# Modulation blocks loaded from GpSimd's queue, a second buffer in the third mixer's stage, and their sums spread anew over VectorE's program

## The chip, the core and the metric

The program runs on one core of a Trainium2 chip. The metric is the device time of one execution in microseconds; before the change it was 1848.09 us, the median of three runs (1843.42, 1848.1 and 1848.09).

## The reference

A sequence of 256 latent tokens (width 1024) goes through two blocks of two layers each. Only layer code of the first block matters here. 256 context tokens go with it in its first layer; the second layer drops their output.

```python
mod = c_silu @ ada_w + ada_b                     # one row for the latents
mod_c = cctx_silu @ ada_w + ada_b                # one row for the context
shift, scale, gate = jnp.split(mod, 3, axis=-1)
hx = rmsnorm(x, norm_w) * (1 + scale) + shift
px = split_cols(hx @ w_in)
ya = global_gqa(...)          # mixer A
yb = neighbourhood_attn(...)  # mixer B
yc_ = window_gqa(...)         # mixer C
ux = concatenate([ya, yb, yc_]) * silu(px[9])
x = x + gate * (ux @ w_out)
```

Everything is float32. The second block (a SwiGLU, two sparse attentions, a merge, a SwiGLU, twice) isn't touched.

## The kernel before

TensorE multiplies float32 operands as two halves: ScalarE rounds a weight panel to a high part (`round_half`, L1019), VectorE subtracts it for the low part (`split_half`, L1581), and three products give the result. A panel is 128x2048 floats (1 MB); raw, high and low panels have two buffers each. SyncE's queue loads the raw panels in order; each load waits until the low part of the panel two before it has been made. The order of the work on each engine is written out by hand, and semaphores tie the engines together.

A layer of the first block runs mixer A, B, C. Each has projections (`qkv`), the output product of the mixer before it (`wout`), a gate (`gate`), turns of queries and keys by transposes, and attention.

A modulation tile is 128 of the 3072 columns of `mod`. TensorE makes the 16 tiles of the first layer's shift and scale at the start; the other 32 of both layers (`MOD_TILES`) are made on VectorE. The weights of one tile are a block `modw[i]` of 128x1024 floats (512 KB). A tile takes two sums, one with the latents' row and one with the context's: a multiplication with a running sum over 1024 columns (`mod_sums`, L1743), whose products go to PSUM banks 4 to 7. The rows (`c_rows`, 128x2048) are loaded first and passed through silu by ScalarE (L1212). There are three phases (`MOD_PHASES`): B0 in mixer B of the first layer (tiles 0 to 15), C0 in mixer C of the first layer (16 to 23) and B1 in mixer B of the second layer (24 to 31). `MOD_AT` says how many sums stand at which place of VectorE's program: after the split of a projection panel (`panel1`), between copies of queries and keys (`near0`, `near2`), after a turn by the position tables (`turned1`), after a residual step of `wout` (`out0` to `out3`), in the gate (`gate0`).

Three readers wait for sums. TensorE waits before the turns of C0 (L2877) until all sums of C0 are there, and in attention B (L2683) until those of B are, since both want banks 4 to 7. The residual of mixer A's output product (`wout`, L2163) waits for gates of its layer. TensorE takes a pair of banks again (`take`, L2445) only when the residual of the step two before it has read them. So a residual that is late on VectorE holds TensorE.

The blocks are loaded by SyncE's queue among the panels (`mod_load`, L866): in B0 and B1 in turn into two halves of `token_major`, in C0 into one buffer in `near_bias`, with a wait until the sums of the block that lies there are made. GpSimd's own queue loads the near mixer's bias tables (`near_bias`, L944).

Of the kernel before, what the change touches and what calls it, by code (L numbers as in the profile page):

```python
# [29 lines left out]
ALU = mybir.AluOpType  # L30
# [3 lines left out]
P = 128  # L34
D = 1024
KT = D // P
T = 256
# [28 lines left out]


MOD_AT = {("B", 0): {"near0": (0, 3), "panel1": (3, 6), "panel2": (6, 8), "near2": (8, 11), "panel3": (11, 14), "panel4": (14, 17),
                     "panel5": (17, 20), "out0": (20, 22), "out1": (22, 24), "out2": (24, 26), "out3": (26, 28),
                     "gate0": (28, 30), "gate1": (30, 32)},  # L70
          ("C", 0): {"panel1": (0, 2), "turned1": (2, 4), "panel2": (4, 6), "turned2": (6, 8), "out0": (8, 10), "out1": (10, 12),
                     "out2": (12, 14), "out3": (14, 16)},
          ("B", 1): {"near0": (0, 1), "panel1": (1, 3), "panel2": (3, 5), "near2": (5, 8), "panel3": (8, 10), "panel4": (10, 13),
                     "panel5": (13, 16)}}
# [242 lines left out]
def program(nc, ctx, xin, smallg, small1, small2, consts, rpb, crows, modw, weights, out):  # L317
# [3 lines left out]
    def sem(name):  # L321
        return ctx.enter_context(nc.semaphore(name))
# [69 lines left out]
    mod_in, mod_sum = [sem(f"modulation_weights_in{i}") for i in range(3)], sem("modulation_sums_done")  # L392
# [168 lines left out]
    def c_rows(m):  # L561

        return tok[:, K1:K1 + 2 * D] if m == "B" else gates[:, :]

    def mod_weights(m, i):

        return tok[:, i % 2 * D:(i % 2 + 1) * D] if m == "B" else bias[:, 0:D]

    def mod_landed(m, i):

        if m == "C":
            return mod_in[2], 16 * (i - MOD_PHASES["C", 0][0] + 1)
# [271 lines left out]
    def _(sp):  # L844
# [22 lines left out]
        def mod_load(m, i):  # L867

            first = MOD_PHASES[m, 0][0] if i < 24 else 24
            held = 2 if m == "B" else 1  # L870
            if i - first >= held:
                sp.wait_ge(mod_sum, 2 * (i - held + 1))
            sp.dma_start(mod_weights(m, i), modw[i]).then_inc(mod_landed(m, i)[0], 16)

        def c_rows_load(m, l):

            if m == "B":
                before = ONE["attnA", l]
                sp.wait_ge(pv, before.at["groups"] + before.groups)
            else:  # L880
                before = ONE["attnB", l]
                sp.wait_ge(omul, before.at["pairs"] + before.pairs)
            row = bass.AP(crows.tensor, crows.offset, [[0, P], [1, 2 * D]])
            sp.dma_start(c_rows(m), row).then_inc(c_rows_in, 16)
            for i in range(2 if m == "B" else 1):
                mod_load(m, MOD_PHASES[m, l][0] + i)

        mod_loads = {}
        for (m, l), counts in (("B", 0), (1, 2, 2, 2, 1, 3, 2, 1)), (("B", 1), (0, 1, 3, 1, 1)), (("C", 0), (0, 2, 3, 2)):
            n, i = ONE["qkv" + m, l].at["panels"] + 2, MOD_PHASES[m, l][0] + (2 if m == "B" else 1)  # L890
            for k, count in enumerate(counts):
                mod_loads[n + k] = [(m, i + j) for j in range(count)]
                i += count
            assert i == MOD_PHASES[m, l][1], (m, l, i)

        for n in range(ADA_FIRST + 1, START2["panels"] + 2):
            before = 4 if n == ADA_FIRST + 1 else n - 2
            for m, l in MOD_PHASES:
                if before == ONE["qkv" + m, l].at["panels"] + 2:
                    c_rows_load(m, l)  # L900
            freed_panel(before)
            sp.dma_start(raw_of(n, 0, PAN), weights[n]).then_inc(loaded[n % 2], 16)
            for m, i in mod_loads.get(before, ()):
                mod_load(m, i)
# [28 lines left out]
    def _(pool):  # L933
# [10 lines left out]
        def near_bias(l, i):  # L944
# [7 lines left out]
                pool.wait_ge(mod_sum, 2 * MOD_PHASES["C", 0][1])  # L952
            pool.dma_start(near_buffer(i % 3), rpb[l * NPAIR * TT + i]).then_inc(bias_in[i % 3], 16)

        def add_a(k, j):

            pool.wait_ge(sqa_ready, now(sqa_ready, 4 * (k - 1) + j + 1))
            pool.tensor_tensor(squares_a(0), squares_a(0), squares_a(j), ALU.add).then_inc(pool_chain, 1)
            pool.wait_ge(pool_chain, chain.next())
# [6 lines left out]
            pool.tensor_tensor(squares_b(0), squares_b(0), squares_b(j), ALU.add).then_inc(pool_chain, 1)  # L966
            pool.wait_ge(pool_chain, chain.next())

        for i in range(NPAIR * TT):
            near_bias(0, i)  # L970
        near_bias(1, 0)
        near_bias(1, 1)
        add_a(1, 1)
# [12 lines left out]
        for kt in range(KT):  # L986
            half = x_normed(kt)[:, T:2 * T]
            pool.tensor_tensor(half, half, invb, ALU.mult).then_inc(ctx_ready, 1)
        for i in range(2, NPAIR * TT):
            near_bias(1, i)  # L990
        assert chain.n == POOL_ENTRY, chain.n
# [579 lines left out]
    def _(dve):  # L1571
# [12 lines left out]
        def split_panel(n):  # L1584
            split_half(n, 0)
            split_half(n, 1)
# [143 lines left out]
        def mod_sums(m, l, a, b):  # L1730


            for x in range(a, b):
                i, v = MOD_PHASES[m, l][0] + x // 2, x % 2
                layer, tile = MOD_TILES[i]
                if x == 0:
                    dve.wait_ge(c_rows_silu, 2 * (list(MOD_PHASES).index((m, l)) + 1))
                dve.wait_ge(*mod_landed(m, i))
                add = sm1[:, layer * NSMALL1 + SMALL1["ada_b"][0] + tile:layer * NSMALL1 + SMALL1["ada_b"][0] + tile + 1]
                to = mod[:, layer * 48 + 2 * tile + v:layer * 48 + 2 * tile + v + 1]  # L1740
                if x >= 2:
                    dve.wait_ge(mod_sum, 2 * MOD_PHASES[m, l][0] + x - 1)
                dve.tensor_tensor_reduce(mod_products(x), mod_weights(m, i), c_rows(m)[:, v * D:(v + 1) * D], 1.0, add,  # L1743
                                         ALU.mult, ALU.add, to).then_inc(mod_sum, 1)

        def second_scale():

# [234 lines left out]
        for l in range(LAYERS):  # L1982
# [153 lines left out]
            def wout(m):  # L2136
# [7 lines left out]
                for q in range(4):  # L2144
# [1272 lines left out]
```

## Time and profile before

| | before |
|---|---|
| median of three runs | 1848.09 us |
| the profiled execution, its own time | 1844.76 us |
| its span | 1842.9 us |
| TensorE busy | 1783.7 us (97%) |
| VectorE busy | 1343.7 us (73%) |
| ScalarE busy | 1084.0 us (59%) |
| GpSimd busy | 54.4 us (3%) |
| granted TensorE clock, mean of the span | 0.992 |

Around the span lie 1.9 us of the execution's time. Read such a table with care: TensorE counts as busy while a matmul runs at whatever clock, so its idle time is only the part of the loss that shows at once. Each phase of the modulation covers a short part of the span: B0 lies between 130 and 236 us, C0 between 279 and 351 us, B1 between 504 and 566 us.

### The profile page before, as it was taken

Reading aid. Unit: us, or ns where it says so; the run is one execution under the profiler, and the core shown is the slowest. Engines: PE = TensorE matmul, PEld = TensorE weight load, DVE = VectorE, ACT = ScalarE, POOL = GpSimd, SP = SyncE. Lnnn points to the kernel's source line nnn. Section 1 sums busy time; section 2 is a strip of 40 time slices with the busy share of each in tenths; the row PEclk is TensorE's granted clock in tenths of the full one; section 3 lists DMA queues with packets and bytes.
Section 4 is the critical chain, followed back from the end, with each engine's and each line's share of the span. In section 5 each row is a group of like instructions: output and inputs, shape, how many; then the busy total and the mean of one; then the engine's idle time right before and its main releaser. Section 6 shows DMA issues by size and latency. Waiting matters only on the chain.

```text
span 1842.9 us, 33652 instructions
## 1 busy us (share of the span) xinstructions
PE 1783.7 (97%) x12856; PEld 1552.3 (84%) x12856; DVE 1343.7 (73%) x2410; ACT 1084.0 (59%) x1897; POOL 54.4 (3%) x56
## 2 busy tenths in 40 slices
PE   7999989889999999999999999999999999999998
PEld 5878867669888888888889988889888888998887
DVE  6766774677866668776688787767776679788765
ACT  5463273285735477764557667755775546667762
POOL 0000000003000000000000000000000000000001
PEclk9999999899999999999999999999999999999999
DMA  8214423301254314555533445545555643355553
GB/s 346 102 70 171 172 81 137 126 25 70 102 191 155 115 70 160 190 197 193 199 137 116 160 174 191 184 182 191 197 182 183 232 145 109 137 183 183 184 185 134
DMA packets 45241, 288.36 MB, mean 156 GB/s; under 512 B 5232, under 2 KB 6640, under 8 KB 13760
## 3 DMA queue, kind: packets, MB, share of 16 engines
q1 hardware_dynamic: 43568, 281.38, 42.4%
q0 software_dynamic: 1552, 5.29, 0.9%
q8 instruction: 85, 1.39, 0.3%
q14 instruction: 36, 0.29, 0.0%
HBM read 285.60 MB, written 1.05 MB: 156 GB/s over the span
## 4 chain that ended last, share of the span: by engine, by line
PE 73%; ACT 4%; DVE 3%; issue 2%; DMA 0%; POOL 0%; DVEq 0%; ACTq 0%
PE bank L2439 25%; PE bank L2440 13%; PE bank L2433 10%; PE bank L2435 9%; PE bank L2434 9%; PE bank L2732 2%; PE bank L2678 2%; ACT work L1163 1%; PE bank L2630 1%; ACT token_major L1142 1%; PE bank L2615 1%; DVE panels_lo L1581 1%; ACT panels_hi L1019 0%; ACT softmax_stats L1162 0%; DMA token_major<-modw 0%
## 5 line engine op out<-in xcount | busy, mean ns | idle before, releaser
L2439 PE MATMUL bank<-acts,panels_hi 128*128 128x512 f32 x2032 | 707.6, 395 | 0.8 <-DVE panels_lo L1581 0.8
L1581 DVE TENSOR_TENSOR panels_lo<-raw_panels,panels_hi 128x1024 fp32r<-128x1024 f32 x468 | 573.0, 1242 | 165.5 <-ACT panels_hi L1019 163.6
L1019 ACT ACTIVATE panels_hi<-raw_panels 128x1024 fp32r<-128x1024 f32 x468 | 484.0, 1054 | 260.7 <-PE bank L2435 164.7
L2440 PE MATMUL bank<-acts,panels_lo 128*128 128x256 f32 x2032 | 563.5, 277 | 0.0
L2439 PEld LDWEIGHTS bank<-acts,panels_hi 128*128 128x128 f32 x2032 | 381.1, 188 | 90.6 <-DVE panels_lo L1581 1.6
L2440 PEld LDWEIGHTS bank<-acts,panels_lo 128*128 128x128 f32 x2032 | 381.5, 188 | 0.2
L2433 PE MATMUL bank<-acts,panels_hi 128*128 128x256 f32 (+1 forms) x1120 | 353.7, 316 | 11.1 <-DVE xT L2163 8.3
L2434 PE MATMUL bank<-acts,panels_hi 128*128 128x256 f32 (+1 forms) x1120 | 347.6, 310 | 0.0
L2435 PE MATMUL bank<-acts,panels_lo 128*128 128x256 f32 (+1 forms) x1120 | 347.3, 310 | 0.0
L2433 PEld LDWEIGHTS bank<-acts,panels_hi 128*128 128x128 f32 x1120 | 215.1, 192 | 30.3 <-DVE xT L2163 9.1
L2435 PEld LDWEIGHTS bank<-acts,panels_lo 128*128 128x128 f32 x1120 | 214.9, 192 | 11.1
L2434 PEld LDWEIGHTS bank<-acts,panels_hi 128*128 128x128 f32 x1120 | 215.0, 192 | 10.3
L2433 PE MATMUL bank<-panels_hi,acts 128*128 128x256 f32 (+1 forms) x528 | 182.8, 346 | 1.2 <-DVE kT_split L2113 0.6
L2435 PE MATMUL bank<-panels_hi,acts 128*128 128x256 f32 (+1 forms) x528 | 179.2, 339 | 0.0
L2434 PE MATMUL bank<-panels_lo,acts 128*128 128x256 f32 (+1 forms) x528 | 178.8, 339 | 0.0
L1163 ACT ACTIVATE work<-bank,softmax_stats 128x512 f32<-128x512 f32 (+2 forms) x240 | 129.4, 559 | 31.2 <-DVE softmax_stats L1858 26.3
L2220 DVE TENSOR_TENSOR work<-bank,work 128x512 f32<-128x512 f32 x88 | 60.8, 691 | 93.5 <-ACT work L1388 93.5
L2433 PEld LDWEIGHTS bank<-panels_hi,acts 128*128 128x128 f32 x528 | 100.5, 190 | 16.1 <-issue 2.3
L2435 PEld LDWEIGHTS bank<-panels_hi,acts 128*128 128x128 f32 x528 | 100.3, 190 | 11.1
L2434 PEld LDWEIGHTS bank<-panels_lo,acts 128*128 128x128 f32 x528 | 100.6, 190 | 10.4
L1388 ACT ACTIVATE work<-bank 128x512 f32<-128x512 f32 x88 | 52.7, 599 | 59.3 <-PE bank L2440 49.8
L2732 PE MATMUL bank<-token_major 128*64 128x128 f32 (+1 forms) x1120 | 87.4, 294 | 0.0
(301 smaller groups left out, 1914.5 us busy)
## 6 DMA issues: line engine op xcount, KB each, us to landing
raw_panels<-weights SPq DMA_DIRECT2D x236, 1024.0 KB, 4.8
token_major<-modw SPq DMA_DIRECT2D x24, 512.0 KB, 4.4
token_major<-weights SPq DMA_DIRECT2D x4, 1024.0 KB, 8.9
near_bias<-modw SPq DMA_DIRECT2D x8, 512.0 KB, 3.6
near_bias<-rpb POOLq DMA_DIRECT2D x12, 256.0 KB, 3.5
xT<-xin SPq DMA_DIRECT2D x4, 512.0 KB, 5.5
gates<-weights SPq DMA_DIRECT2D x2, 1024.0 KB, 9.8
near_bias<-weights SPq DMA_DIRECT2D x4, 512.0 KB, 7.1
```

What stands on the lines that cost most here:

```text
L1019: act.activation(slot_hi(n, a, b), raw_of(n, a, b), ACT.Copy).then_inc(hi_ready, 1)
L1163: x = act.activation(probs(u)[:, c:c + w], score_bank(u, st)[:, c:c + w], ACT.Exp, bias=stat(u, k, 1), scale=1.0 if blk == 1 and un.bias i ...
L1388: act.activation(tile4(up_rest(j), 2), step_rest(s), ACT.Copy).then_inc(rest_out, 1)
L1581: dve.tensor_tensor(slot_lo(n, a, b), raw_of(n, a, b), slot_hi(n, a, b).bitcast(F32), ALU.subtract).then_inc(lo_ready, 1)
L2220: dve.tensor_tensor(tile4(gu, 2), step_main(s), tile4(up_rest(j), 2), ALU.add).then_inc(freed, 1)
L2433: pe.matmul(dst, whi_, xhi_, start=start, stop=False, skip_group_check=True)
L2434: pe.matmul(dst, whi_, xlo_, start=False, stop=False, skip_group_check=True)
L2435: return pe.matmul(dst, wlo_, xhi_, start=False, stop=stop, skip_group_check=True)
L2439: pe.matmul(bank.rearrange("p (c t) -> p c t", c=2), whi_, with_rest(xhi_), start=start, stop=False, skip_group_check=True)
L2440: return pe.matmul(bank[:, 0:T], wlo_, xhi_, start=False, stop=stop, skip_group_check=True)
L2678: o = pe.matmul(to, q[a], keys[b], start=k + a + b == 0, stop=a == 1, skip_group_check=True)
L2732: o = pe.matmul(out_bank(blk, st, step.pair)[e * HD:(e + 1) * HD, q0:q0 + n], v, probsT(g)[:, c:c + n], start=start, stop=k >= len(step.ad ...
```

## The change

Four edits. The loads of `c_rows` and of all blocks `modw[i]` leave SyncE's queue for GpSimd's: one function issues the rows and then the phase's blocks, each from the third on behind a wait for the sums of the block two before it. In C0 the odd blocks land in a second buffer: columns 128 to 383 of the four 512-column groups of `token_major` at V1, which mixer C's values (columns 0 to 127) leave free. Such a load writes four pieces of 256 floats to a partition, and the sums read them in the same form. `MOD_AT` has new counts in C0 and B1. In mixer B's `wout`, the turn of mixer C's keys (`rotate(2)`) comes ahead of the sums of `out2`. In B0 only the name of a place changes: two sums of `gate1` join those of `gate0`, with nothing between them. No computation is added or dropped.

```diff
-          ("C", 0): {"panel1": (0, 2), "turned1": (2, 4), "panel2": (4, 6), "turned2": (6, 8), "out0": (8, 10), "out1": (10, 12),
-                     "out2": (12, 14), "out3": (14, 16)},
+          ("C", 0): {"panel0": (0, 4), "panel1": (4, 5), "turned1": (5, 8), "panel2": (8, 9), "out0": (9, 12), "out1": (12, 13),
+                     "out2": (13, 14), "out3": (14, 16)},
...
-        return tok[:, i % 2 * D:(i % 2 + 1) * D] if m == "B" else bias[:, 0:D]
+        if m == "B":
+            return tok[:, i % 2 * D:(i % 2 + 1) * D]
+        if i % 2:
+            return tok[:, V1:V1 + 2048].rearrange("p (t c) -> p t c", t=4)[:, :, P:P + T]
+        return bias[:, 0:D].rearrange("p (t c) -> p t c", t=4)
...
-            held = 2 if m == "B" else 1
-            if i - first >= held:
-                sp.wait_ge(mod_sum, 2 * (i - held + 1))
-            sp.dma_start(mod_weights(m, i), modw[i]).then_inc(mod_landed(m, i)[0], 16)
...
+        def modulation_loads(m, l):
+
+            if m == "B":
+                before = ONE["attnA", l]
+                pool.wait_ge(pv, before.at["groups"] + before.groups)
+            else:
+                before = ONE["attnB", l]
+                pool.wait_ge(omul, before.at["pairs"] + before.pairs)
+            row = bass.AP(crows.tensor, crows.offset, [[0, P], [1, 2 * D]])
+            pool.dma_start(c_rows(m), row).then_inc(c_rows_in, 16)
+            first, last = MOD_PHASES[m, l]
+            for i in range(first, last):
+                if i >= first + 2:
+                    pool.wait_ge(mod_sum, 2 * (i - 1))
+                to = mod_weights(m, i)
+                pool.dma_start(to, modw[i] if m == "B" else modw[i].rearrange("p (t c) -> p t c", t=4)).then_inc(mod_landed(m, i)[0], 16)
...
-        for i in range(NPAIR * TT):
+        near_bias(0, 0)
+        near_bias(0, 1)
+        modulation_loads("B", 0)
+        for i in range(2, NPAIR * TT):
             near_bias(0, i)
+        modulation_loads("C", 0)
         near_bias(1, 0)
         near_bias(1, 1)
...
+                    if m == "B" and q == 2:
+                        rotate(2)
                     if m != "C":
                         sums_at("BC"["AB".index(m)], f"out{q}")
-                    if m == "B" and q == 2:
-                        rotate(2)
```

The changed kernel is nine lines shorter, so its lines have other numbers: the sums L1735 for L1743, the splits L1570 for L1581, the residuals L2154 for L2163.

The first place is VectorE in C0, around the first two residuals of mixer B's output product. A sum is a row that writes `bank,modulation` and the row under it that reads the running sum out. Before:

```order
L1743 ISA bank,modulation<-near_bias,gates,small_sb 128x1024
L1743 ISA modulation 128x1
L1743 ISA bank,modulation<-near_bias,gates,small_sb 128x1024
L1743 ISA modulation 128x1
L2163 SCALAR_TENSOR_TENSOR xT<-bank,modulation,xT 128x256 x4
L1743 ISA bank,modulation<-near_bias,gates,small_sb 128x1024
L1743 ISA modulation 128x1
L1743 ISA bank,modulation<-near_bias,gates,small_sb 128x1024
L1743 ISA modulation 128x1
L2163 SCALAR_TENSOR_TENSOR xT<-bank,modulation,xT 128x256 x4
L1581 TENSOR_TENSOR panels_lo<-raw_panels,panels_hi 128x1024 x2
```

And now:

```order
L1570 TENSOR_TENSOR panels_lo<-raw_panels,panels_hi 128x1024 x2
L1735 ISA bank,modulation<-near_bias,gates,small_sb 128x1024
L1735 ISA modulation 128x1
L2154 SCALAR_TENSOR_TENSOR xT<-bank,modulation,xT 128x256 x4
L1735 ISA bank,modulation<-near_bias,gates,small_sb 128x1024
L1735 ISA modulation 128x1
L1735 ISA bank,modulation<-token_major,gates,small_sb 128x1024
L1735 ISA modulation 128x1
L1735 ISA bank,modulation<-token_major,gates,small_sb 128x1024
L1735 ISA modulation 128x1
L2154 SCALAR_TENSOR_TENSOR xT<-bank,modulation,xT 128x256 x4
L1570 TENSOR_TENSOR panels_lo<-raw_panels,panels_hi 128x1024 x2
```

Between the split and the first residual stood four sums (two more stand above the rows shown) and now stands one; behind the residual two have become three.

The second place is VectorE at the end of B1, where mixer A's output product of the second layer begins. Before:

```order
L1581 TENSOR_TENSOR panels_lo<-raw_panels,panels_hi 128x1024 x2
L1743 ISA bank,modulation<-token_major,small_sb 128x1024
L1743 ISA modulation 128x1
L1743 ISA bank,modulation<-token_major,small_sb 128x1024
L1743 ISA modulation 128x1
L1743 ISA bank,modulation<-token_major,small_sb 128x1024
L1743 ISA modulation 128x1
L2163 SCALAR_TENSOR_TENSOR xT<-bank,modulation,xT 128x256 x4
```

And now:

```order
L1735 ISA bank,modulation<-token_major,small_sb 128x1024
L1735 ISA modulation 128x1
L1570 TENSOR_TENSOR panels_lo<-raw_panels,panels_hi 128x1024 x2
L2154 SCALAR_TENSOR_TENSOR xT<-bank,modulation,xT 128x256 x4
L1570 TENSOR_TENSOR panels_lo<-raw_panels,panels_hi 128x1024 x2
L2154 SCALAR_TENSOR_TENSOR xT<-bank,modulation,xT 128x256 x4
```

The three sums in front of the residuals are gone; they stand behind earlier panels.

The third place is GpSimd's program in C0, now:

```order
L920 DMA near_bias<-rpb 128x512 x2
L931 DMA gates<-crows 128x2048
L937 DMA near_bias<-modw 128x1024
L937 DMA token_major<-modw 128x4x256
L937 DMA near_bias<-modw 128x1024
L937 DMA token_major<-modw 128x4x256
```

Before, the two bias loads ahead of these rows were followed at once by the second layer's bias loads, and the same eight blocks went by SyncE's queue between panels:

```order
L884 DMA gates<-crows 128x2048
L873 DMA near_bias<-modw 128x1024
L902 DMA raw_panels<-weights 128x2048 x2
L873 DMA near_bias<-modw 128x1024 x2
L902 DMA raw_panels<-weights 128x2048
L873 DMA near_bias<-modw 128x1024 x3
```

SyncE's queue now holds nothing but panels there.

## Rows read from the trace of the kernel before

**Rows 1.** Waits of TensorE, whole span: line, releaser, us, times, longest
```profile
PE bank L2433 <- DVE xT L2163: 8.3, 3, 5.0
```
**Rows 2.** Timeline of TensorE: start, length, what [idle before, releaser]
```profile
235.37 0.50 PE L2433 MATMUL bank<-acts,panels_hi 128*128 128x512 f32 x1 [2.31 <-DVE modulation L1743]
...
308.50 0.40 PE L2433 MATMUL bank<-acts,panels_hi 128*128 128x512 f32 x1
...
319.18 0.39 PE L2435 MATMUL bank<-acts,panels_lo 128*128 128x512 f32 x1
324.54 0.79 PE L2433 MATMUL bank<-acts,panels_hi 128*128 128x512 f32 x1 [4.97 <-DVE xT L2163]
...
343.08 0.39 PE L2435 MATMUL bank<-acts,panels_lo 128*128 128x512 f32 x1
350.42 1.94 PE L2615 MATMUL bank<-consts_sb,token_major 128*128 128x128 f32 x8 [6.96 <-issue]
...
538.69 0.50 PE L2433 MATMUL bank<-panels_hi,acts 128*128 128x512 f32 x1 [0.56 <-DVE kT_split L2113]
...
566.75 0.39 PE L2433 MATMUL bank<-acts,panels_hi 128*128 128x256 f32 x1 [2.98 <-DVE xT L2163]
```
**Rows 3.** Windows: stretch, length, TensorE busy (instructions), granted clock, DMA, GB/s
```profile
328.00:329.00 1.00, 1.00 (x4) 0.50 0.00 0
329.00:330.00 1.00, 1.00 (x5) 0.74 0.08 29
...
353.00:354.00 1.00, 1.00 (x5) 0.79 0.54 188
```
**Rows 4.** Timeline of VectorE in C0
```profile
298.76 2.36 DVE L1581 TENSOR_TENSOR panels_lo<-raw_panels,panels_hi 128x1024 fp32r<-128x1024 f32 x2 [8.95 <-ACT panels_hi L1019]
...
310.88 2.36 DVE L1581 TENSOR_TENSOR panels_lo<-raw_panels,panels_hi 128x1024 fp32r<-128x1024 f32 x2 [0.41 <-ACT panels_hi L1019]
...
320.41 1.29 DVE L1743 CUSTOM_DVE_ANT_0 bank<-near_bias,gates,small_sb 128x1024 f32<-128x1024 f32 x1 [3.60 <-issue]
...
322.83 1.66 DVE L2163 SCALAR_TENSOR_TENSOR xT<-bank,modulation,xT 128x256 f32<-128x256 f32 x4
...
341.31 0.42 DVE L2039 TENSOR_TENSOR work<-token_major,consts_sb 128x256 f32<-128x256 f32 x1
...
343.92 1.66 DVE L2163 SCALAR_TENSOR_TENSOR xT<-bank,modulation,xT 128x256 f32<-128x256 f32 x4 [0.21 <-DVE work L2070]
...
350.18 0.14 DVE L1743 DVE_READ_ACCUMULATOR2_ANT modulation<- 128x1 f32 x1
```
**Rows 5.** Timeline of SyncE's queue in C0
```profile
316.83 12.47 SPq L873 DMA_DIRECT2D near_bias<-modw  x3
```
**Rows 6.** Timeline of ScalarE in C0
```profile
289.68 2.01 ACT L1212 ACTIVATE gates<-gates 128x1024 f32<-128x1024 f32 x2
...
338.12 2.01 ACT L1019 ACTIVATE panels_hi<-raw_panels 128x1024 fp32r<-128x1024 f32 x2 [16.46 <-PE bank L2435]
```
**Rows 7.** Timeline of VectorE in B0 (first row) and B1
```profile
149.29 0.14 DVE L1743 DVE_READ_ACCUMULATOR2_ANT modulation<- 128x1 f32 x1
...
530.41 0.14 DVE L1743 DVE_READ_ACCUMULATOR2_ANT modulation<- 128x1 f32 x1
...
534.94 1.29 DVE L1743 CUSTOM_DVE_ANT_0 bank<-token_major,small_sb 128x1024 f32<-128x1024 f32 x1 [0.38 <-DMA token_major<-modw]
...
565.82 1.85 DVE L2163 SCALAR_TENSOR_TENSOR xT<-bank,modulation,xT 128x256 f32<-128x256 f32 x4
```
**Rows 8.** View of the tensor modw: its 32 loads of 512 KB
```profile
DMA to landing us min/median/max: 3.4/3.7/6.2
```
**Rows 9.** View of the tensor rpb: its 16 loads of 256 KB by GpSimd
```profile
DMA to landing us min/median/max: 2.8/3.0/5.1
```
**Rows 10.** DMA issues: name, queue, count, KB each, median us to landing
```profile
token_major<-weights SPq DMA_DIRECT2D x2, 512.0 KB, 12.5
```
**Rows 11.** View of line L2022, which reads `token_major` in such pieces: ns
```profile
L2022 DVE TENSOR_TENSOR token_major<-token_major,head_stats x6: 691/694/1226, 49.8 to 470.8; 128x512 f32<-128x512 f32 x4, 128x1024 f32<-128x1024 f32 x2
```

More of the change, by code:

```diff
@@ L68 @@
 MOD_AT = {("B", 0): {"near0": (0, 3), "panel1": (3, 6), "panel2": (6, 8), "near2": (8, 11), "panel3": (11, 14), "panel4": (14, 17),
-                     "panel5": (17, 20), "out0": (20, 22), "out1": (22, 24), "out2": (24, 26), "out3": (26, 28),
-                     "gate0": (28, 30), "gate1": (30, 32)},
-          ("C", 0): {"panel1": (0, 2), "turned1": (2, 4), "panel2": (4, 6), "turned2": (6, 8), "out0": (8, 10), "out1": (10, 12),
-                     "out2": (12, 14), "out3": (14, 16)},
-          ("B", 1): {"near0": (0, 1), "panel1": (1, 3), "panel2": (3, 5), "near2": (5, 8), "panel3": (8, 10), "panel4": (10, 13),
-                     "panel5": (13, 16)}}
+                     "panel5": (17, 20), "out0": (20, 22), "out1": (22, 24), "out2": (24, 26), "out3": (26, 28), "gate0": (28, 32)},
+          ("C", 0): {"panel0": (0, 4), "panel1": (4, 5), "turned1": (5, 8), "panel2": (8, 9), "out0": (9, 12), "out1": (12, 13),
+                     "out2": (13, 14), "out3": (14, 16)},
+          ("B", 1): {"near0": (0, 1), "panel1": (1, 4), "panel2": (4, 7), "near2": (7, 10), "panel3": (10, 13), "panel4": (13, 16)}}
 QKV_PANELS = {"A": 3, "B": 6, "C": 3}
@@ L391, in program @@
     c_rows_in, c_rows_silu = sem("c_rows_in"), sem("c_rows_silu")
-    mod_in, mod_sum = [sem(f"modulation_weights_in{i}") for i in range(3)], sem("modulation_sums_done")
+    mod_in, mod_sum = [sem(f"modulation_weights_in{i}") for i in range(4)], sem("modulation_sums_done")
     scale_ready = sem("second_scale_ready")
@@ L565, in mod_weights @@
     def mod_weights(m, i):
-        return tok[:, i % 2 * D:(i % 2 + 1) * D] if m == "B" else bias[:, 0:D]
+        if m == "B":
[3 more added lines that the diff above has]
+        return bias[:, 0:D].rearrange("p (t c) -> p t c", t=4)
     def mod_landed(m, i):
         if m == "C":
-            return mod_in[2], 16 * (i - MOD_PHASES["C", 0][0] + 1)
+            return mod_in[2 + i % 2], 16 * ((i - MOD_PHASES["C", 0][0]) // 2 + 1)
         return mod_in[i % 2], 16 * ((i if i < 16 else i - 8) // 2 + 1)
@@ L865, in freed_panel @@
                 sp.wait_ge(lo_ready, now(lo_ready, 2 * split_index(n) + 2))
-        def mod_load(m, i):
-            first = MOD_PHASES[m, 0][0] if i < 24 else 24
-            held = 2 if m == "B" else 1
-            if i - first >= held:
-                sp.wait_ge(mod_sum, 2 * (i - held + 1))
-            sp.dma_start(mod_weights(m, i), modw[i]).then_inc(mod_landed(m, i)[0], 16)
[L875 to L894, printed above, removed]
-        for n in range(ADA_FIRST + 1, START2["panels"] + 2):
[L897 to L901, printed above, removed]
+        for n in range(ADA_FIRST + 1, START2["panels"] + 2):
+            freed_panel(4 if n == ADA_FIRST + 1 else n - 2)
             sp.dma_start(raw_of(n, 0, PAN), weights[n]).then_inc(loaded[n % 2], 16)
-            for m, i in mod_loads.get(before, ()):
-                mod_load(m, i)
         cmp0, kv0 = TWO["cmp_kv"].at["panels"], TWO["nsa_kv"].at["panels"]
@@ L988, in _ @@
             pool.tensor_tensor(half, half, invb, ALU.mult).then_inc(ctx_ready, 1)
+        modulation_loads("B", 1)
         for i in range(2, NPAIR * TT):
@@ L1742, in mod_sums @@
                     dve.wait_ge(mod_sum, 2 * MOD_PHASES[m, l][0] + x - 1)
-                dve.tensor_tensor_reduce(mod_products(x), mod_weights(m, i), c_rows(m)[:, v * D:(v + 1) * D], 1.0, add,
-                                         ALU.mult, ALU.add, to).then_inc(mod_sum, 1)
+                products, row = mod_products(x), c_rows(m)[:, v * D:(v + 1) * D]
+                if m == "C":
+                    products, row = (y.rearrange("p (t c) -> p t c", t=4) for y in (products, row))
+                dve.tensor_tensor_reduce(products, mod_weights(m, i), row, 1.0, add, ALU.mult, ALU.add, to).then_inc(mod_sum, 1)
         def second_scale():
```

## The prediction

> **What bounds the kernel now.** I read the waits of TensorE first, since it is busy for nearly the whole span and every stretch in which it stands still is time. Its longest group of waits on work that this change touches is that on the residuals: 8.3 us in three waits, 5.0 the longest [rows 1]. The timeline of TensorE says where they lie and shows the others. In C0 it finishes the second step of mixer B's output product at 319.18 + 0.39 = 319.57 and goes on at 324.54: 4.97 us for a residual. It finishes the first half of the gate at 343.08 + 0.39 = 343.47 and turns at 350.42: 6.96 us, which that view puts down to no releaser (the turns wait for the last sum). In B1 it waits 2.98 us up to 566.75 for a residual and 0.56 us up to 538.69 for a copy of keys; at the end of B0 it waits 2.31 us up to 235.37 for the last sum [rows 2]. Second, the granted clock: it stands at 0.50 (the 1.2 GHz level) after each of the two long waits and comes back within the slices that read 0.74 and 0.79 [rows 3]. So slow work runs from 324.54 to about 329.5 and from 350.42 to about 353.4; at half the speed this costs 5.0 / 2 = 2.5 us and 3.0 / 2 = 1.5 us. A matmul of 512 columns has 0.79 us in the record behind the first wait, against 0.40 before it [rows 2].
>
> Third, what VectorE does meanwhile. In C0 it idles 8.95 us ahead of the split at 298.76, while at 320.41 it stands 3.60 us for a load that stood behind two sums: there is one buffer, the load can be issued only at 316.83, and it lands 3.6 us later [rows 4, 5]. The residual that TensorE wants then starts at 322.83. So C0 isn't short of VectorE; it does its sums late, in front of residuals, and in series with their loads. What would be needed is that residuals and turns find their data, and the rows say by how much they don't.
>
> **C0, walked with the new order.** Two sums take 322.83 - 320.41 = 2.42 us, a residual of four instructions 1.66, a panel's split 2.36, and the turn of keys up to the next residual 343.92 - 341.31 = 2.61 [rows 4]. Silu of the rows ends at 289.68 + 2.01 = 291.7 [rows 6]. Four sums then fit before 298.76: 291.7 + 4.8 = 296.5. They cost nothing; the 8.95 us of idle time hide them. From the end of that split to the next split at 310.88 stood four sums and the turn of queries; now stand four sums and the turn. Same work, so the split is at 310.88 as before and ends at 313.2. One sum ends at 314.4. The first step of the output product runs from 308.50, and two steps take until 319.57, so it is done at 314.1. The residual runs 314.4 to 316.1, which is 3.5 us before TensorE asks. The wait of 4.97 us goes, and with it the drop of the clock that follows it.
>
> What is late next? Three sums end at 319.7, the second residual 321.4, a split 323.7, one sum 324.9. TensorE ends its third step at 319.57 + 5.5 = 325.0. Third residual 326.7, turn of keys 329.3, one sum 330.5. The fourth step ends at 343.47 - 4.97 - 2.5 - 5.5 = 330.5. Last residual 332.2; the split needs ScalarE's rounding, which starts when TensorE has let the panel go (338.12 in the old run, 330.6 now) and has its first half after a microsecond, so it isn't late [rows 6]. Split 334.5, two sums 336.9. The old run turned 0.24 us after its last sum was read out at 350.18 [rows 2, 4], so the turns now start at 337.2. TensorE reaches them at 343.47 - 7.47 = 336.0. It still waits 1.2 us. After the waits of 2.31 and 2.98 us the records show matmuls of 0.50 and 0.39 us and not 0.79, so I take no drop of the clock for 1.2 us. C0 gives 350.42 - 337.2 = 13.2, and 1.5 for the second drop: 14.7 us.
>
> **B1.** Three sums (3.6 us) leave the place ahead of the residual at 565.82 [rows 7]. It can start at 562.2, half a microsecond ahead of TensorE's stop at 566.75 - 2.98 = 563.8 if two instructions, 0.9 us, suffice for the first step. The 2.98 us go. The sums go where VectorE idles behind earlier panels, as in C0. One place gets tighter: the sum at 534.94 now belongs to a block whose load waits for the sum read out at 530.41. If L is the time from that read-out to landing, the sum starts at 530.5 + L. At L = 4.5 that is the old time; each microsecond above it lengthens the old wait of 0.56 us. I take L = 5.0 and 0.5 us. B1 gives 2.5 us.
>
> **B0.** Its order is the same to the row. The last sums stand behind a split that waits for TensorE, so the wait of 2.31 us stays: 0.
>
> **The moved loads.** SyncE's queue loses 32 blocks and 3 loads of rows. It gains nothing that counts: TensorE lost no time on a raw panel in these stretches. The unknown is L, a block of 512 KB issued by GpSimd. By SyncE such a block took 3.4 to 6.2 us, median 3.7 [rows 8]; GpSimd's loads of half the size took 2.8 to 5.1, median 3.0 [rows 9]. Below, 3.0 is the end: L can't be shorter than for half the bytes. Above, the farthest row of 512 KB is 12.5 us, where it stood behind other loads [rows 10]. I take 5.0, near 3.7 with something for the other queue and for a panel of 1 MB that is often on its way at that moment. Between 3.0 and 7.8 C0's sum doesn't change. Its third block is asked for after the second sum, at 294.1, and wanted behind the split at 301.1; its fifth is asked for after the sixth sum, two sums and 0.4 us of idle time ahead of the split at 310.88 [rows 4], so at 308, and is due by 319.57 - 1.66 - 1.2 = 316.7, or TensorE waits again. At L = 7.8 the third comes 0.8 late and the fifth just in time. GpSimd itself has no other work in these three stretches but the bias loads that stood behind the last sum before too. For the row pieces of 1 KB in the second buffer no row exists; they count in L.
>
> The Trainium skill (DMA: Bandwidth & Descriptors, section Anatomy of one DMA) fits a load on GpSimd's path as about 2.0 us plus the bytes over 436 GB/s. By it L is an estimated 3.2 us, B1 would gain 3.4 and the sum would be 18.1 us. The trace has 3.0 for half the bytes, where the fit has 2.6, so I keep the longer L.
>
> **The form of the new operands.** The sums read four pieces of 256 floats. An instruction on 1024 floats in such pieces took 1226 ns [rows 11], where a split of contiguous ones takes 2.36 / 2. Nothing is added; at worst 0.05 us for each of 16 sums.
>
> **The sum.** 14.7 + 2.5 + 0 = 17.2 us. The profiled execution took 1844.76 us, which gives 1827.6. It lies 3.3 us below the median of the runs shown; from their mean, 1846.5, the sum gives 1829.3. I predict 1829.
>
> **The rivals.**
> 1. *The loads land late, at L of 7 to 8 us.* For it: no row shows a block of this size on this queue, and four pieces to a partition are new. Against: 5.1 us at most for half the bytes [rows 9]. B1's copy of keys then holds TensorE 8 - 4.5 = 3.5 us longer, which eats that gain; C0 stays. Gain 14.7 + 2.98 - 3.5 = 14.2: 1832.
> 2. *C0's second wait moves and doesn't go.* The last sums, the last residual and a split make 1.66 + 2.36 + 2.42 = 6.4 us between TensorE's step and its turns, against 5.5 us of its own work. Anything late on VectorE in this chain comes back one to one. If it is late by half of what the old wait was, 3.5 us and a drop of the clock of 1.5 come back: gain 12.2. If what the turns free is then lost in attention C, which I can't walk with these rows, 8.5 us in all go and 8.7 are left: 1838.
> 3. *Slower: VectorE starves for blocks.* One mechanism: block i + 2 can be asked for only when block i is summed, so each buffer turns in L + 2.4 us. In B0 the first block is summed at 149.3 [rows 7], and seven turns and the last pair end at 149.3 + 7 (L + 2.4) + 2.4. That passes the old end, 235.2, when L passes 9.5 us. At L = 12.5 [rows 10] B0 ends at 256, 21 us late. In C0 the third block lands at 306.6, its second sum ends at 313.5 behind the turn of queries, and the fifth block lands at 326, where the old residual started at 322.83; so C0 is some 4 us slower than before, and B1 gains nothing: 1846.5 + 25 = 1871. It decides from about L = 10.5, where B0 loses 7 us and C0 still keeps its second wait of 7. For it in the trace: nothing, as all 16 loads landed by 5.1 us [rows 9]. The Trainium skill (SBUF — State Buffer, section SBUF: two separate sides) says that GpSimd can't write its descriptors while VectorE runs a copy in a two-port mode; that would be a way to such an L.
> 4. *Almost nothing comes of it* (both waits of C0 return with other releasers, for instance a silu that waits for rows which land late): gain about 3, 1843.
>
> **Chances.** Forecast 0.73 (1823 to 1834), rival 1 0.11, rival 2 0.09, rival 4 0.04, rival 3 0.03. The runs before lie between 1843.4 and 1848.1, so from the lowest less a gain of 20 to the highest less a gain of 10 the range is 1823 to 1838, which takes in rivals 1 and 2 and leaves out less than 2 in 10; I set its lower end at 1822. A measurement of this kernel tells 0.3% (5.5 us) from no change: faster 0.93, same 0.04, slower 0.03.
>
> **What would show it.** In C0, TensorE goes through 319 to 325 with no wait, its granted clock stays at 1.00, and its wait in front of the turns is 1 to 2 us, ending near 337. VectorE's sums start at 292. In B1 the wait for the residual is gone and one of about 1 us stands at 538. The wait at 235 is as before. GpSimd's blocks land in 4 to 6 us. Behind C0 everything comes 13 to 15 us earlier, behind B1 17, and that distance stays to the end. The prediction is wrong if the blocks take over 8 us, if a new wait of over 2 us stands between 279 and 351, or if the lead after C0 melts away in attention C.

## The result, and the profile after

The changed kernel takes 1826.9 us (median of 4 runs, 1822.1 to 1827.9) against 1846.5 (median of 4, 1843.4 to 1848.1) in the runs beside it. The ratio is 0.9891, 95% interval 0.9867 to 0.9914: about 19.6 us less, where 17.2 were forecast and 1829 was given. The profiled execution took 1822.07 us with a span of 1820.3, and is the fastest of the four.

The waits of TensorE over the whole span, which answer to [rows 1]:

```profile
PE bank L2424 <- DVE modulation L1735: 2.3, 1, 2.3
...
PE bank L2606 <- DVE kT_split L1748: 1.1, 1, 1.1
PE bank L2606 <- issue: 1.1, 1, 1.1
...
PE bank L2424 <- DVE kT_split L2104: 0.4, 1, 0.4
PE bank L2424 <- DVE xT L2154: 0.3, 1, 0.3
```

The 8.3 us on residuals (L2163 before, L2154 now) are 0.3, and the 7.0 us ahead of the turns are 1.1. The 2.3 us at the end of B0 stand as they were. TensorE's timeline, which answers to [rows 2], at the end of B0, through the place in C0 where it stood for 4.97 us, ahead of the turns, and at the copy of keys in B1:

```profile
235.57 0.50 PE L2424 MATMUL bank<-acts,panels_hi 128*128 128x512 f32 x1 [2.31 <-DVE modulation L1735]
...
319.58 0.39 PE L2424 MATMUL bank<-acts,panels_hi 128*128 128x512 f32 x1
...
335.67 0.39 PE L2426 MATMUL bank<-acts,panels_lo 128*128 128x512 f32 x1
337.16 1.07 PE L2606 MATMUL bank<-consts_sb,token_major 128*128 128x128 f32 x8 [1.10 <-issue]
...
522.10 0.50 PE L2424 MATMUL bank<-panels_hi,acts 128*128 128x512 f32 x1 [0.41 <-DVE kT_split L2104]
```

No idle time stands at the row of 319.58, nor at any from 311 to 325. The turns start at 337.16; the walk in the prediction had put them at 337.2. Eight turns last 1.07 us where the same group lasted 1.94 behind the long wait of before. The clock over three such stretches (length, TensorE busy and instructions, granted clock, DMA share, GB/s), to be read beside [rows 3]:

```profile
231.00:236.00 5.00, 2.69 (x17) 1.00 0.56 210
319.00:325.00 6.00, 6.00 (x28) 1.00 0.69 190
334.00:342.00 8.00, 6.90 (x36) 1.00 0.58 200
```

VectorE in C0, which answers to [rows 4]: first sum, first residual, second residual, third split, last read-out.

```profile
291.90 1.29 DVE L1735 CUSTOM_DVE_ANT_0 bank<-near_bias,gates,small_sb 128x1024 f32<-128x1024 f32 x1 [1.91 <-ACT gates L1201]
...
301.21 1.29 DVE L1735 CUSTOM_DVE_ANT_0 bank<-near_bias,gates,small_sb 128x1024 f32<-128x1024 f32 x1
...
314.54 1.65 DVE L2154 SCALAR_TENSOR_TENSOR xT<-bank,modulation,xT 128x256 f32<-128x256 f32 x4
...
319.78 1.66 DVE L2154 SCALAR_TENSOR_TENSOR xT<-bank,modulation,xT 128x256 f32<-128x256 f32 x4
321.36 2.35 DVE L1570 TENSOR_TENSOR panels_lo<-raw_panels,panels_hi 128x1024 fp32r<-128x1024 f32 x2
...
336.91 0.14 DVE L1735 DVE_READ_ACCUMULATOR2_ANT modulation<- 128x1 f32 x1
```

The residual that started at 322.83, after TensorE had stopped, now starts at 314.54, five microseconds before TensorE wants it. The third block's sum follows the split at 301.21 with no wait. Four pieces to a partition cost the sums nothing: 1.29 us as before.

How far the changed kernel is ahead at one and the same point of the program is called its lead here. GpSimd is a good place to read it from, since it has instructions at fixed points. Of before, the second norm's first addition, the first bias load of attention B in the second layer, and an addition near the end:

```profile
424.43 2.25 POOL L958 TENSOR_TENSOR work<-work 128x512 f32<-128x512 f32 x1 [72.75 <-ACT work L1317]
...
584.27 0.54 POOL L953 DMA_DIRECT2D near_bias<-rpb  x1 [17.69 <-DVE softmax_stats L1845]
...
1809.37 2.20 POOL L958 TENSOR_TENSOR work<-work 128x512 f32<-128x512 f32 x1 [363.53 <-DVE work L1907]
```

and of the changed kernel the same three:

```profile
409.65 2.25 POOL L942 TENSOR_TENSOR work<-work 128x512 f32<-128x512 f32 x1 [71.20 <-ACT work L1306]
...
564.43 0.54 POOL L920 DMA_DIRECT2D near_bias<-rpb  x1 [25.80 <-DVE softmax_stats L1836]
...
1786.69 2.20 POOL L942 TENSOR_TENSOR work<-work 128x512 f32<-128x512 f32 x1 [361.92 <-DVE work L1898]
```

The lead is 14.78 us at the second norm, 19.84 at the attention behind B1, 21.07 at 1240 (a row of the same kind) and 22.68 at 1809. It was -0.20 at the end of B0 (235.63 and 235.83), so C0 gives 14.98. Where B1 begins, it has to be read from an engine whose program is the same there, since the loads that open B1 are called by two different engines. ScalarE's first rounding of a panel in B1, before and after:

```profile
507.69 2.01 ACT L1019 ACTIVATE panels_hi<-raw_panels 128x1024 fp32r<-128x1024 f32 x2 [1.79 <-PE bank L2435]
```
```profile
491.25 2.01 ACT L1008 ACTIVATE panels_hi<-raw_panels 128x1024 fp32r<-128x1024 f32 x2 [1.79 <-PE bank L2426]
```

A lead of 16.44, so B1 gives 19.84 - 16.44 = 3.40. The other three steps, 1.66 + 1.23 + 1.61 = 4.50 us, lie where nothing was changed. They are drops of the granted clock (at 431, 674 and 1507) in the one profiled execution of before, which that of after doesn't have. Windows of before, then of after, where the first of them lies:

```profile
432.00:433.00 1.00, 1.00 (x7) 0.50 0.00 0
...
434.00:435.00 1.00, 1.00 (x8) 0.50 0.71 90
```
```profile
430.00:435.00 5.00, 5.00 (x44) 1.00 0.59 210
```

So the two profiled executions differ by 22.7 us, of which 18.2 belong to the change; the medians differ by 19.6.

Last, the loads themselves, by their tensor (calls by GpSimd with their durations, who waited, landing):

```profile
L937 POOL DMA_DIRECT2D token_major<-modw x28: 528/528/763, 130.8 to 527.1; - x28
...
who waited for it (us, times):
  DVE bank L1735: 1.4, 2
...
DMA to landing us min/median/max: 3.8/4.3/6.7
```

This answers to [rows 8] (3.4, 3.7, 6.2 by SyncE). VectorE waited 1.4 us for blocks in all.

### The profile page after: what moved, and what is told of

Read it like the earlier page. It is cut to its first block, busy times and chain, and to the rows that moved or that the text cites. A ratio compares the mean times of both kernels' runs of the same rounds, so it can differ in the third digit from the quotient of the medians.

```text
span 1820.3 us, 33652 instructions
## 1 busy us (share of the span) xinstructions
PE 1774.7 (97%) x12856; PEld 1545.7 (85%) x12856; DVE 1343.2 (74%) x2410; ACT 1083.4 (60%) x1897; POOL 74.0 (4%) x91
## 4 chain that ended last, share of the span: by engine, by line
PE 87%; ACT 6%; DVE 4%; issue 3%; DMA 1%; POOL 0%; SPq 0%; DVEq 0%; ACTq 0%
PE bank L2430 26%; PE bank L2424 13%; PE bank L2431 13%; PE bank L2426 13%; PE bank L2425 13%; ACT work L1152 2%; PE bank L2723 2%; PE bank L2669 2%; ACT token_major L1131 1%; PE bank L2621 1%; DVE panels_lo L1570 1%; PE bank L2606 1%; ACT panels_hi L1008 1%; DVE bank L1735 1%; PE bank L2529 1%
## 5 line engine op out<-in xcount | busy, mean ns | idle before, releaser
L1570 DVE TENSOR_TENSOR panels_lo<-raw_panels,panels_hi 128x1024 fp32r<-128x1024 f32 x468 | 573.2, 1243 | 156.3 <-ACT panels_hi L1008 154.3
L2425 PEld LDWEIGHTS bank<-panels_lo,acts 128*128 128x128 f32 x528 | 100.2, 190 | 10.1
```

The source lines that it names most:

```text
L1570: dve.tensor_tensor(slot_lo(n, a, b), raw_of(n, a, b), slot_hi(n, a, b).bitcast(F32), ALU.subtract).then_inc(lo_ready, 1)
L2425: pe.matmul(dst, whi_, xlo_, start=False, stop=False, skip_group_check=True)
```

## The experiments

Two theories were at hand. A: C0's gain has two parts, the second buffer (which takes away the wait for a residual and the drop of the clock behind it) and the new places of the sums (which shorten the wait ahead of the turns); B1's is its new spread; the queue gives nothing. Against it: the queue is what counts, because SyncE's waits no longer hold up the panels; or the spread alone would have done it. The kernel before ran beside them at 1847.0 us (first four below) and at 1847.9 (the other four).

**The second buffer with the sums in their old places in C0.**

```diff
-"panel0": (0, 4), "panel1": (4, 5), "turned1": (5, 8), "panel2": (8, 9), "out0": (9, 12), "out1": (12, 13), "out2": (13, 14), ...
+"panel1": (0, 2), "turned1": (2, 4), "panel2": (4, 6), "turned2": (6, 8), "out0": (8, 10), "out1": (10, 12), "out2": (12, 14), ...
```
(and the turn of keys behind the sums again)

> The changed kernel with the old counts of C0 and the old place of the turn of keys; second buffer, GpSimd's queue and the new counts of B1 stay. Theory A (the two waits of C0 had two causes, the series of load and sum, and sums in front of residuals): the buffer alone takes away the first wait (4.97 us and its drop of the clock), since the residual then starts near 318, but the last sum still comes near 341.5, so TensorE waits 5 to 6 us in front of the turns. About 4.5 us slower than the changed kernel, or 6 with a drop of the clock: 1831 to 1833. Rival B (the second buffer is the whole change in C0): as fast as the changed kernel, 1827. Rival C (the spread is the whole): as slow as the kernel before less B1's 3 us, 1843.

1832.3 us (1830.9 to 1832.9), ratio 0.9918 [0.9902, 0.9935]. TensorE's waits from 125 to 580:

```profile
PE bank L2606 <- issue: 5.3, 1, 5.3
...
PE bank L2424 <- DVE modulation L1735: 2.3, 1, 2.3
```

No wait for a residual is left; that ahead of the turns is 5.3 of its 7.0. The buffer alone takes the first wait away. The new places, with the turn of keys moved ahead of the sums, give the other 5.4 us (1832.3 - 1826.9): a wait longer by 4.2 us, and the clock at 0.50 behind it from 342 to 347. The intervals of the two ratios overlap, so the size isn't sure. What the turn of keys gives by itself was not run.

**The new places with one buffer.**

```diff
-        if i % 2:
-            return tok[:, V1:V1 + 2048].rearrange("p (t c) -> p t c", t=4)[:, :, P:P + T]
...
-                if i >= first + 2:
-                    pool.wait_ge(mod_sum, 2 * (i - 1))
+                held = 2 if m == "B" else 1
+                if i >= first + held:
+                    pool.wait_ge(mod_sum, 2 * (i - held + 1))
```

> The changed kernel with one buffer in C0: each block is asked for only when the one before it is summed. Theory A: each of the seven later blocks costs its 4.3 us from the call to landing in VectorE's row; walked through, the first residual of mixer B's output product starts near 325 and TensorE waits 6 to 7 us there, and the turns start near 352. C0 is then as slow as before or 2 us slower; only B1's 3 us stay: 1843 to 1846. Rival C (the spread gives the gain): within 3 us of the changed kernel, 1827 to 1830.

1842.5 us (1840.4 to 1845.4), 0.9977 [0.9968, 0.9987], half a microsecond below what was expected:

```profile
PE bank L2423 <- DVE xT L2153: 8.8, 2, 6.6
...
PE bank L2605 <- issue: 3.5, 1, 3.5
```

VectorE waited 18.5 us for blocks, in eight places, of which seven with 17.3 us lie in C0. In series with their loads the sums in front of the second split come so late that the residual is later than in the old order (6.6 for 5.0 us). The wait ahead of the turns is shorter (3.5 for 7.0), but the other two, 6.6 and 2.2, take it back: C0's waits are 12.3 us where they were 11.9. So the two parts of theory A don't stand side by side, the new places need the buffer. Without it they give C0 nothing: of the 4.5 us, B1's new spread alone gives as much (below).

**All loads back on SyncE**, called behind the panels, with everything else as changed.

```diff
+        for (m, l), counts in (("B", 0), (1, 2, 2, 2, 1, 3, 2, 1)), (("B", 1), (0, 2, 2, 2)), (("C", 0), (2, 2, 2)):
...
-        modulation_loads("B", 0)
-        modulation_loads("C", 0)
-        modulation_loads("B", 1)
```

> The changed kernel with all loads of rows and blocks back in SyncE's queue, placed between panels so that no panel load stands behind an unmet wait for sums; VectorE, TensorE and ScalarE run the same program as in the changed kernel. Theory A (the queue buys nothing, only the second buffer and the spread do): the same time within 1 us, turns at 337, blocks landing in about 3.7 us instead of 4.3. Rival D (the free queue is part of the gain): 2 to 5 us slower, with waits of VectorE for blocks or of ScalarE for panels.

1824.3 us (1823.8 to 1830.2), 0.9885 [0.9865, 0.9905], an interval that lies over that of the changed kernel.

```profile
PE bank L2439 <- DVE modulation L1750: 2.3, 1, 2.3
PE bank L2621 <- issue: 1.1, 1, 1.1
```

The same two waits of the same length; the blocks land in 3.3, 4.2 and 6.6 us (least, median, most), where 3.7 was expected as the median, and VectorE waits 4.8 us for two of them, without a wait of TensorE behind it. The median is 2.6 us below that of the changed kernel where 1 was expected at most. GpSimd's queue gives nothing that can be measured.

**The queue alone**: blocks by GpSimd, but one buffer in C0 and the sums in their old places in C0 and B1 (the edits of the first two, and the counts of B1 of before).

> The kernel before with only the queue changed: GpSimd issues rows and blocks, one buffer in C0, old counts. Theory A: each block that VectorE waits for comes 0.6 us later (4.3 against 3.7 us), four such waits in C0, so the time is 0 to 2.5 us above the kernel before: 1846 to 1849. Rival D: 2 us or more faster than the kernel before.

1848.1 us (1846.2 to 1851.3), 1.0008 [0.9998, 1.0017]:

```profile
PE bank L2424 <- DVE xT L2154: 9.4, 2, 6.4
PE bank L2606 <- issue: 8.1, 1, 8.1
```

Both waits of C0 are longer than in [rows 2], by 1.4 and 1.1 us (of the 9.4, 6.4 lie in C0 and 3.0 in B1): with one buffer each load is on the path. The blocks landed in 3.9 us in the median, not in the 4.3 that were expected. Alone the queue gives nothing, and may cost a microsecond. Together with the run before, the rival theory of the queue falls.

**B1 with its old spread.**

```diff
-("B", 1): {"near0": (0, 1), "panel1": (1, 4), "panel2": (4, 7), "near2": (7, 10), "panel3": (10, 13), "panel4": (13, 16)}}
+("B", 1): {"near0": (0, 1), "panel1": (1, 3), "panel2": (3, 5), "near2": (5, 8), "panel3": (8, 10), "panel4": (10, 13), "panel5": (13, 16)}}
```

> The changed kernel with the old counts of B1 alone: three sums stand again in front of the first residual of mixer A's output product in the second layer. Theory A: the wait of 3.0 us before that residual comes back, and the copy of keys no longer waits for a block. 3.0 us slower than the changed kernel, 4.5 where the clock drops behind the wait: 1829 to 1831. Rival: the gain of B1 came from clock drops that are chance, and the time stays within 1 us of 1827.

1831.5 us (1830.9 to 1834.3), 0.9915 [0.9896, 0.9935], half a microsecond above what was expected. The wait is back to the hundredth, and the clock falls behind it (timeline; then windows of a microsecond, of 551 to 555):

```profile
549.72 0.39 PE L2425 MATMUL bank<-acts,panels_hi 128*128 128x256 f32 x1 [2.98 <-DVE xT L2155]
```
```profile
552.00:553.00 1.00, 1.00 (x7) 0.50 0.00 0
553.00:554.00 1.00, 1.00 (x6) 0.50 0.44 74
```

B1's spread is worth 4.6 us by the medians, against a wait of 2.98; the two intervals overlap here too. The profile of before has no such drop behind its own 2.98 us (its clock is 1.00 from 566 to 572), so part of what the spread saves is a drop that comes in some executions only. Another part need not belong to the spread at all: this profile also took 3.0 us more than that of the changed kernel in a later stage that is the same in both (last section). The two profiles of before and after, which have neither, put B1 at 3.4 us.

**The sums ahead of the waits.** The two waits that are left both stand behind a split whose input TensorE's own progress lets through late. Here two of the last four sums of B0, and the last two of C0, go in front of that split.

```diff
-"out3": (26, 28), "gate0": (28, 32)}
+"out3": (26, 30), "gate0": (30, 32)}
...
+                    if (m, l, q) == ("B", 0, 3):
+                        sums_at("C", "out3")
                     if q == 1 or q == 3 and m != "C":
                         split_panel(st.at["panels"] + q // 2 + 2)
...
-                    if m != "C":
+                    if m != "C" and (m, l, q) != ("B", 0, 3):
```

> The changed kernel with two places moved: in B0 two sums go from the gate, where TensorE waits 2.3 us for the last of four, to the stretch behind the last residual, where VectorE idles 4 to 5 us; in C0 the last two sums go in front of the last split, which TensorE needs only 5 us later. Theory A: both waits go, 2.3 + 1.1 = 3.4 us, and with the first the drop of the clock at 235 that four other runs had behind it (1.7 us): 1822 to 1824. Rival E: the last split, 2.4 us later, and ScalarE's panel behind it hold TensorE inside the gate of C0 instead, and C0 gains nothing: 1824 to 1825. Rival F: in B0 the two last sums wait for their block: B0 gains nothing.

1822.4 us (1818.6 to 1823.0), 0.9862 [0.9844, 0.988]. The three windows that were shown of the changed kernel:

```profile
231.00:236.00 5.00, 5.00 (x27) 1.00 0.74 262
319.00:325.00 6.00, 6.00 (x28) 1.00 0.74 233
334.00:342.00 8.00, 8.00 (x44) 1.00 0.54 195
```

TensorE is busy through all three. The gain over the changed kernel is 4.5 us by the medians, for waits of 2.3 and 1.1; the intervals of the two ratios overlap, so its size isn't sure, but that both waits are gone is, and behind C0 this profile is 3.5 us ahead of that of the changed kernel. It is the fastest version run on GpSimd's queue.

**The same on SyncE's queue** (the edits of the third and the last together).

> The two moved places of the kernel above together with SyncE's queue for all rows and blocks. Theory A: both waits gone as there; the queue adds nothing but the 0.4 us of B1's wait for a block: within 1 us of the kernel above, 1821 to 1824. Rival: a panel load stands behind a wait for sums in the new order, and ScalarE waits for a panel: 2 us or more slower than the kernel above.

1821.7 us (1818.9 to 1823.9), 0.9861 [0.9842, 0.988]: no different from the last, as the queue gave nothing before.

**Loads made late.** To find what the changed order bears, GpSimd writes a scratch tile seven times (some 3.6 us in all) ahead of each block from the third on.

```diff
+                for _ in range(DELAYS if i >= first + 2 else 0):
+                    pool.memset(slow[:, :], 0.0).then_inc(pool_slow, 1)
+                    slowed[0] += 1
+                    pool.wait_ge(pool_slow, slowed[0])
```

> The changed kernel with seven memsets of a scratch tile on GpSimd between the wait and the call of each block from the third of a phase on: each block is asked for some 3.5 us later, so L, from the sum's read-out to landing, is near 7.8 instead of 4.4. Theory P (as predicted: C0 is safe up to L = 7.8, B1 pays L - 4.5): only the copy of keys in B1 waits, 3.4 us longer: 1830 to 1831. Theory Q (VectorE has no idle time left in C0 between 311 and 337, so its slack for the fifth block is only the 5.0 us between the call at 308.3 and the sum at 313.3): C0 pays what L exceeds 5.0 as well, partly twice since later blocks are asked for late; 3 to 6 us there, the turns near 342, and B1's 3.4: 1833 to 1837. Rival 3 of the prediction says B0 is safe below L = 9.5: its last sum stays at 235 within 1 us.

1842.9 us (1837.5 to 1847.3), 0.9971 [0.9958, 0.9985]: 16 us of the 19.6 are gone, more than either of the two theories on record for it had (1831 and 1837 at most). B0's last sum, which was to stay at 235 within 1 us, comes just ahead of TensorE's restart at 238.82. TensorE's waits, and VectorE's in C0 for blocks:

```profile
PE bank L2433 <- DVE kT_split L2113: 5.3, 3, 3.1
PE bank L2615 <- issue: 4.1, 1, 4.1
...
PE bank L2433 <- DVE xT L2163: 3.1, 3, 2.1
PE bank L2433 <- DVE modulation L1744: 2.9, 1, 2.9
```
```profile
306.75 1.29 DVE L1744 CUSTOM_DVE_ANT_0 bank<-near_bias,gates,small_sb 128x1024 f32<-128x1024 f32 x1 [0.65 <-DMA near_bias<-modw]
...
321.43 1.29 DVE L1744 CUSTOM_DVE_ANT_0 bank<-near_bias,gates,small_sb 128x1024 f32<-128x1024 f32 x1 [3.02 <-DMA near_bias<-modw]
...
328.02 1.29 DVE L1744 CUSTOM_DVE_ANT_0 bank<-token_major,gates,small_sb 128x1024 f32<-128x1024 f32 x1 [2.46 <-DMA token_major<-modw]
```

All three stages pay. B0: TensorE goes on at 238.82 in place of 235.57, from a start 0.67 us earlier, so 3.9 us are lost, and the clock is at 0.50 behind it from 239 to 242. C0: from its load of rows (284.24, 279.43) to the turns (347.41, 337.16) it loses 10.25 - 4.81 = 5.4 us, with another drop behind it from 347 to 352. B1: the wait for a copy of keys comes back with 3.1 us. One reservation: the delays stand in series on GpSimd, so a block called right behind another is late by more than 3.6 us. The block that landed at 306.75 had its buffer free at 299.13 (7.6 us), the one at 321.43 at 313.65 (7.8 us), the one at 328.02 at 316.06 (12.0 us).

## Why the prediction held, point by point

- *C0, the walk.* Right: 14.98 us for 14.7. First sum 291.9 (291.7), second split 311.06 (310.88), first residual 314.54 (314.4), turns 337.16 (337.2), wait 1.10 (1.2). The runs with one of the two edits show what each does: the buffer alone takes the first wait away, and the new places shorten the second only together with it.
- *B1.* The mechanism was right, the term mis-sized: 3.4 us in the profiles for 2.5, and 4.6 between medians with the old spread put back. The wait of 2.98 went whole. What was wrong is L = 5.0 and its 0.5 us. At the tight place the sum was read out at 513.97, GpSimd's call began at 514.42, and the block was there at 518.34: L = 4.4, and the wait for the copy of keys is 0.41 where 1.1 were forecast. That is 0.65 of the 0.9 us; the rest comes where the wait of 2.98 stood, and what it is stays open.
- *B0.* Right: the wait of 2.31 us stands. That it could be taken away by order alone, the prediction didn't ask.
- *The moved loads.* Right that SyncE's queue gains nothing that counts. The L of 4.4 lies between the 3.7 of SyncE and the 5.0 that was taken. The blocks landed in 3.8 to 6.7 us, where the signs had 4 to 6. The fit of the Trainium skill (DMA: Bandwidth & Descriptors, section Anatomy of one DMA), an estimated 3.2 us for 512 KB, lies below the shortest landing seen, 3.8 us on GpSimd's queue; the measurement decides, 1.1 us more in the median, and L has another 0.4 us ahead of the call.
- *What the order bears.* Wrong, where it did no harm: the prediction had "Between 3.0 and 7.8 C0's sum doesn't change", and B0 safe up to L = 9.5. In the run with late loads the third block came 0.65 us late, as was worked out for 7.8 (0.8). The fifth had L = 7.8 as well, and the first residual behind it was still in time (it starts at 322.64, and TensorE has no wait before 332.15). But the walk stopped there. VectorE had waited 3.0 us for this block, has no idle time of over 0.3 us from 313 to 337 in the changed kernel, and so keeps the delay up to the last sum; the sixth block, with its L of 12.0, adds 2.5. Together that is what the turns lost, 5.4 us. The prediction's own remark, that anything late on VectorE in this chain comes back one to one, holds from the fifth block on. For B0 the estimate let each buffer turn freely and asked only when the last pair ends; in truth each block has a place in the order. VectorE stood for 10.1 us in six places there, the first of them (1.7 us, at 156.52) behind an L of some 7.7, and TensorE got 3.9 of them. How much L alone the order bears can't be told exactly from this run, since its delays add up. Rival 1's "C0 stays" at L of 7 to 8 was too mild: some 3 us more, so about 1835, an estimate from the fifth block alone that leaves out B0.
- *The rivals.* Rival 1 and 3 need late loads: VectorE waited 1.4 us in all, and no block took longer than 6.7 us to land, so nothing here shows the way to a long L that rival 3 names. Rival 2 is excluded by the turns at 337.16, rival 4 by the same row. By the time alone rival 1 (1832) could hardly be told from the forecast, since the four runs spread over 5.9 us; it is the waits that tell them apart.
- *The clock.* Right for the long waits, and incomplete for the others. That no drop comes after the waits of 2.31 and 2.98 us was read from one execution. Behind the same wait of 2.3 us at the end of B0 the clock stays at 1.00 in three profiles (before, after, the old spread in B1) and falls in four; behind the 3.0 us of B1 it stays in one and falls in two. From TensorE's restart at 235.37 to the first wait in the attention behind it, at 243.60, the profile of before takes 8.2 us; where the clock falls (one buffer, 235.32 to 245.16) it takes 9.8. So such a wait costs its length and sometimes 1.6 us more. This was not in the sum, and can be a part of what the medians gained above 17.2. That the lead stays to the end didn't hold in the profiles, by the three drops of before.
- *The number.* C0 and B1 give 18.4 us in the profiles for 17.2; the other 1.2 of the 19.6 are no more than one chance drop does to a run. B1's 3.4 is also what the prediction worked out beside its sum with L = 3.2. That is luck: L was 4.4.

## What to carry to other kernels

When sums and their loads stand in series in front of something that the busiest engine waits for, give the load a second buffer first (some 10 us here by medians: 14.7 less B1's 4.6) and move the work afterwards (5.4 us); moving without the buffer made one wait longer and gained nothing in that stage. Work that nobody waits for belongs ahead of an instruction that is itself waiting for the busy engine, not behind it. And walk a slack through to the end of the stage, since what is late at one place is late at all that follow on that engine.

## What the runs showed of the hardware

- The granted clock drops in some executions without a wait of TensorE in front of it: at 431 to 435 of before (rows above; TensorE busy without a gap from 422), at 1507 to 1510 in the same profile (0.56, 0.50 and 0.50, TensorE busy throughout), at 914 to 918 in the last run on SyncE's queue. A third drop of before, at 674 to 678, stands behind two microseconds in which TensorE was busy for 0.3. The three of before cost 1.2 to 1.7 us each by the leads above; the profile of after holds none. The Trainium skill (TensorE: Matmul & The Clock Gate, section Part 1: The HAM clock gate) says of the number of slow matmuls at a start that "it's run-variable"; the runs agree in that, though it speaks of starts and of idle gaps and not of such stretches.
- A stage can be slower at a full clock. From ScalarE's rounding at 697.30 to that at 849.44 the changed kernel takes 152.1 us, with TensorE busy throughout and the clock at 1.00. Three of the ten profiles (the queue alone, the old spread in B1, late loads) take 3.0 us more for it, also busy throughout and at 1.00 (155.1, from 701.57 to 856.71 with the old spread in B1); the program is the same there. What it comes from stays open. It is as large as the effects that were looked for, so a difference of a few microseconds between two medians needs the profile beside it.
- The clock behind one and the same 2.3 us wait isn't the same in all executions (a window from 236 to 238 of before, then of the first experiment):

```profile
236.00:238.00 2.00, 2.00 (x11) 1.00 0.36 131
```
```profile
236.00:238.00 2.00, 2.00 (x6) 0.50 0.43 131
```

- A DMA call costs GpSimd 0.53 us for a contiguous block and 0.76 for one whose partitions are written in four pieces. In C0 the pieces also land later by about as much or a little more: 4.2, 4.2 and 4.3 us from the call for the last three, against 3.8, 3.9 and 3.9 for the contiguous blocks between them.
- A block of 512 KB landed 0.6 us later from GpSimd after the change than from SyncE before (4.3 and 3.7 in the median). The queue makes little of it: with the changed order SyncE's took 4.2, and with the old order GpSimd's took 3.9. So the order of the loads, or what else is on its way with them, makes 0.4 to 0.5 us, and the queue 0.1 to 0.2.
